# Odd mixer: a pair's two heads scored alternately from the two halves of the array's rows, values stationary and scaled probabilities moving

## The reference, cut to what matters

```python
def odd_mixer(xn, w_in, w_o, cos_f, sin_f):
    hcat = (xn @ w_in).reshape(b, s, DIL_GROUPS, 3, DIL_HEADS, HEAD_DIM)
    q = apply_rope(hcat[:, :, :, 0], cos_f, sin_f)
    k = apply_rope(hcat[:, :, :, 1], cos_f, sin_f)
    v = hcat[:, :, :, 2]
    return dilated_attention(q, k, v) @ w_o
# dilated_attention, per group: sc = q.k * HEAD_DIM**-0.5 where the key is in the
# window, e = exp(sc - m), z = sum e, o = (e / z) v, lse = m + log z;
# out = sum over the groups of softmax(lse) * o
```

## Time and profile before

| | |
|---|---|
| device time, median of 3 runs | 1459.98 us |
| profiled execution, span from the first instruction to the last | 1458.9 us; of its own time outside the span nothing is given |
| PE busy | 1340.8 us (92%), 7187 matmuls |
| PEld busy | 1102.4 us (76%) |
| DVE, ACT, POOL busy | 745.2 us (51%), 494.0 us (34%), 77.4 us (5%) |
| chain that ended last | PE 80%, DVE 11%, issue 4%, ACT 3%, DMA 2% |
| mean granted clock of PE | 0.941 of full speed |
| odd mixer's pairs with attention woven in | 975 us to 1208 us |
| attention of the last pair alone | to 1227.8 us |
| output product | 1233.4 us to 1261.1 us |

### The profile page before, as it was taken

One profiled execution on the slowest core, in us unless ns is written; L12 is line 12 of the kernel. 1 busy time (PEld: TensorE's weight loads), 2 busy tenths in 40 slices (PEclk: granted clock), 3 DMA queues, 4 the chain that ended last, 5 costly groups with the idle time before them and its releaser, 6 DMA issues.

```text
span 1458.9 us, 18192 instructions
## 1 busy us (share of the span) xinstructions
PE 1340.8 (92%) x7187; PEld 1102.4 (76%) x7187; DVE 745.2 (51%) x951; ACT 494.0 (34%) x703; POOL 77.4 (5%) x53
## 2 busy tenths in 40 slices
PE   3998997887999997989899999899999998899997
PEld 3645455554999984658489998899999997499996
DVE  4625437834555533143365546666666654365553
ACT  2152010114334332034343333454545444243331
POOL 0000045400000005000000000000000000000000
PEclk9889997769999997977999999999999997999999
DMA  9604374407565553060255563464444433445520
GB/s 330 227 0 146 108 250 156 147 3 216 175 195 172 183 162 76 0 223 8 86 203 183 172 207 102 116 163 130 124 125 124 113 116 130 173 173 177 199 86 29
DMA packets 200060, 208.17 MB, mean 143 GB/s; under 512 B 5339, under 2 KB 166502, under 8 KB 199814
## 3 DMA queue, kind: packets, MB, share of 16 engines
q1 hardware_dynamic: 196992, 201.34, 43.2%
q0 software_dynamic: 992, 3.57, 1.0%
q10 hardware_dynamic: 2022, 2.50, 0.5%
HBM read 206.35 MB, written 2.00 MB: 143 GB/s over the span
## 4 chain that ended last, share of the span: by engine, by line
PE 80%; DVE 11%; issue 4%; ACT 3%; DMA 2%; DVEq 0%; ACTq 0%; SPq 0%
PE bank L1541 16%; PE bank L1542 16%; PE bank L1543 16%; PE bank L1501 6%; PE bank L1400 6%; PE bank L1601 2%; DMA weight_pool<-in_mod_w_dram 2%; PE bank L1389 2%; PE bank L1342 2%; PE bank L1777 1%; PE bank L1660 1%; PE bank L1668 1%; DVE work L1160 1%; PE bank L1677 1%; PE bank L1592 1%
## 5 line engine op out<-in xcount | busy, mean ns | idle before, releaser
L1541 PE MATMUL bank<-hT_high,mlp_up_high 128*128 128x256 f32 x512 | 145.1, 283 | 4.8 <-DVE hT_low L854 4.8
L1543 PE MATMUL bank<-hT_high,mlp_up_low 128*128 128x256 f32 x512 | 144.9, 283 | 0.0
L1542 PE MATMUL bank<-hT_low,mlp_up_high 128*128 128x256 f32 x512 | 144.9, 283 | 0.0
L1541 PE MATMUL bank<-od_w_high,hT_high 128*128 128x384 f32 x384 | 131.8, 343 | 1.7 <-DVE hT_low L854 1.7
L1543 PE MATMUL bank<-od_w_high,hT_low 128*128 128x384 f32 x384 | 129.1, 336 | 0.0
L1542 PE MATMUL bank<-od_w_low,hT_high 128*128 128x384 f32 x384 | 129.0, 336 | 0.0
L854 DVE TENSOR_TENSOR od_w_low<-weight_pool,od_w_high 128x3072 fp32r<-128x3072 f32 x24 | 80.6, 3358 | 53.5 <-ACT od_w_high L544 53.5
L854 DVE TENSOR_TENSOR mlp_down_low<-weight_pool,mlp_down_high 128x2048 fp32r<-128x2048 f32 x32 | 73.3, 2290 | 59.1 <-ACT mlp_down_high L544 59.1
L1541 PEld LDWEIGHTS bank<-hT_high,mlp_up_high 128*128 128x128 f32 x512 | 98.1, 192 | 7.0 <-issue 3.5
L1541 PE MATMUL bank<-hT_high,ffn_up_high 128*128 128x256 f32 x352 | 99.9, 284 | 1.5 <-DVE hT_low L854 1.5
L1541 PE MATMUL bank<-mlp_down_high,hidden_high 128*128 128x512 f32 x256 | 100.3, 392 | 0.0
(11 more groups left out here) (258 smaller groups left out, 2617.8 us busy)
## 6 DMA issues: line engine op xcount, KB each, us to landing
weight_pool<-in_mlp_w_dram SPq DMA_DIRECT2D x64, 1024.0 KB, 7.5
weight_pool<-in_od_w_in_dram SPq DMA_DIRECT2D x72, 512.0 KB, 5.2
weight_pool<-in_mod_w_dram SPq DMA_DIRECT2D x12, 2048.0 KB, 8.1
weight_pool<-in_ffn_w_in_dram SPq DMA_DIRECT2D x44, 512.0 KB, 5.2
weight_pool<-in_ffn_w_out_dram SPq DMA_DIRECT2D x22, 512.0 KB, 6.0
weight_pool<-in_gla_w_in_dram SPq DMA_DIRECT2D x4, 2048.0 KB, 7.9
weight_pool<-in_gla_w_in_dram SPq DMA_DIRECT2D x4, 1024.0 KB, 11.1
weight_pool<-in_gla_w_out_dram SPq DMA_DIRECT2D x2, 2048.0 KB, 8.6
```

The source lines that it names most:

```text
L1541: mm(out_, left[0], right[0], start=start, stop=False, **flag)
L1542: mm(out_, left[0], right[1], start=False, stop=False, **flag)
L1543: return mm(out_, left[1], right[0], start=False, stop=stop, **flag)
```

## The change

- A block of scores now does both heads of one tile: for each of the three key ranges first head 0 (array rows 0 to 63, bank 3), then head 1 (rows 64 to 127, bank 4). Units are renumbered: h = j % 2, t = j // 2. Both banks must be free before a block.
- DVE scales the probabilities in place before they are turned: `od_scale`, a reciprocal of one sum and a multiplication of 128 x 512, with a semaphore `prob_scaled` for which PE's transposes wait.
- In `od_attend` the values of one head (64 columns) are stationary and the turned probabilities (128 columns) move; head 0's result goes to partitions 0 to 63 and head 1's to 64 to 127 of bank 7, so the mixer's result stands with channels on partitions. One call does both heads of a tile; it waits for both turned units. `pv_ps` counts two for a pair, where it counted four.
- `od_out` is one copy of 128 x 256 from bank 7 into `odT`, in the order of the tokens. The transposes of `om`, their copies and the waits for them go; the output product reads `odT`.

```diff
+        odT = view(work, 12800, KD, SEQ)
...
-            def turned_unit(u, j):
+            def turned_unit(u, j, free):
                 act.wait_ge(s["pT_ps"], u + 1)
-                if not isinstance(u, int) or u >= 2:
-                    act.wait_ge(s["pv_ps"], u - 1)
+                if free is not None:
+                    act.wait_ge(s["pv_ps"], free)
...
-                    turned_unit(u + 0, 0)
-                    turned_unit(u + 1, 1)
+                    turned_unit(u + 0, 0, 2 * n + U_OD)
+                    turned_unit(u + 1, 1, 2 * n + U_OD)
                     exp_unit(u + 2, 2, 1, 1.0, od_col(pn, 2))
                     exp_unit(u + 3, 3, 1, 1.0, od_col(pn, 3))
...
-                    turned_unit(u + 2, 2)
-                    turned_unit(u + 3, 3)
+                    turned_unit(u + 2, 2, 2 * n + (U_OD + 1))
+                    turned_unit(u + 3, 3, 2 * n + (U_OD + 1))
...
-            turn_evac(2, oT, dilated)
+            act.wait_ge(s["pv_ps"], U_OD + 2 * OD_PAIRS)
...
-            def od_out(n, par):
-                dve.wait_ge(s["pv_ps"], 4 * n + (U_OD + 4))
-                chain(dve.reciprocal(rinv[:, 32 + 4 * par:36 + 4 * par], rsum[:, 32 + 4 * par:36 + 4 * par]))
-                for t in range(NT):
-                    ins = dve.tensor_tensor(om5[:, t, n, :, :], bank[7][:, P * t:P * t + P].rearrange("p (h d) -> p h d", d=HD),
-                                            rinv[:, 32 + 4 * par + 2 * t:34 + 4 * par + 2 * t].unsqueeze(2).to_broadcast([P, 2, HD]),
-                                            ALU.mult)
-                ins.then_inc(s["o_out"], 1)
+            def od_scale(u, par, j):
+
+                dve.wait_ge(s["prob_ready"], u + 1)
+                col = 32 + 4 * par + j
+                chain(dve.reciprocal(rinv[:, col:col + 1], rsum[:, col:col + 1]))
+                dve.tensor_scalar(prob[:, j % 2, :], prob[:, j % 2, :], rinv[:, col:col + 1], None, ALU.mult)\
+                   .then_inc(s["prob_scaled"], 1)
+
+            def od_out(n):
+                dve.wait_ge(s["pv_ps"], 2 * n + (U_OD + 2))
+                dve.tensor_copy(dilated(odT[:, n, :]), by_sma(bank[7][:, 0:SEQ])).then_inc(s["o_out"], 1)
...
                     od_max(u + 0, 0)
                     od_max(u + 1, 1)
+                    od_scale(u + 0, pn, 0)
+                    od_scale(u + 1, pn, 1)
...
                     od_max(u + 2, 2)
                     od_max(u + 3, 3)
+                    od_scale(u + 2, pn, 2)
+                    od_scale(u + 3, pn, 3)
...
-            def od_scores(u, par, j):
-
-                pe.wait_ge(s["prob_ready"], u - 1)
-                h, t = j // 2, j % 2
-                lo = HD * h
+            def od_scores(u, par, t):
+
+                pe.wait_ge(s["prob_ready"], u)
                 for g, (at, k0, n) in enumerate([(0, 256, 256), (256, 256 + P * t, P), (384, 256 + P * t, P)]):
-                    ins = mm(bank[3 + j % 2][:, at:at + n], qkT[lo:lo + HD, par, g, P * t:P * t + P], qkT[lo:lo + HD, par, g, k0:k0 + n],
-                             start=True, stop=True)
-                ins.then_inc(s["s_ps"], 1)
-
-            def od_attend(u, par, j, n):
-                pe.wait_ge(s["pT_ready"], u + 1)
-                if j == 0:
+                    for h in range(2):
+                        lo = HD * h
+                        ins = mm(bank[3 + h][:, at:at + n], qkT[lo:lo + HD, par, g, P * t:P * t + P], qkT[lo:lo + HD, par, g, k0:k0 + n],
+                                 start=True, stop=True)
+                        if g == 2:
+                            ins.then_inc(s["s_ps"], 1)
+
+            def od_turn_probs(u, j):
+                pe.wait_ge(s["prob_scaled"], u - (U_OD - 1))
+                pe.wait_ge(s["pT_ready"], u - 1)
+                for b in range(4):
+                    ins = pe.transpose(bank[5 + j % 2][:, P * b:P * b + P], prob[:, j % 2, P * b:P * b + P], ident)
+                ins.then_inc(s["pT_ps"], 1)
+
+            def od_attend(u, par, t, n):
+                pe.wait_ge(s["pT_ready"], u + 2)
+                if t == 0:
                     pe.wait_ge(s["o_out"], n + 4)
-                h, t = j // 2, j % 2
                 for b, (g, tile) in enumerate([(0, 0), (0, 1), (1, t), (2, t)]):
-                    ins = mm(bank[7][:, P * t + HD * h:P * t + HD * h + HD], probT[:, j % 2, P * b:P * b + P],
-                             vO[:, par, g, tile, HD * h:HD * h + HD], start=(b == 0), stop=(b == 3))
+                    for h in range(2):
+                        lo = HD * h
+                        ins = mm(bank[7][lo:lo + HD, P * t:P * t + P], vO[:, par, g, tile, lo:lo + HD],
+                                 probT[:, h, P * b:P * b + P], start=(b == 0), stop=(b == 3))
                 ins.then_inc(s["pv_ps"], 1)
...
                     pe.wait_ge(s["qkT_out"], 3 * n + 3)
                     od_scores(u + 0, pn, 0)
-                    od_scores(u + 1, pn, 1)
                 if m is not None:
                     od_turn(m, pm, 0)
                     od_proj(m, pm, 2, 0)
                 if n is not None:
-                    turn_probs(u + 0, 0, u + 1)
-                    turn_probs(u + 1, 1, u + 2)
-                    od_scores(u + 2, pn, 2)
-                    od_scores(u + 3, pn, 3)
+                    od_turn_probs(u + 0, 0)
+                    od_turn_probs(u + 1, 1)
+                    od_scores(u + 2, pn, 1)
                 if m is not None:
                     od_proj(m, pm, 2, 1)
                 if n is not None:
                     od_attend(u + 0, pn, 0, n)
-                    od_attend(u + 1, pn, 1, n)
-                    turn_probs(u + 2, 2, u + 3)
-                    turn_probs(u + 3, 3, u + 4)
+                    od_turn_probs(u + 2, 2)
+                    od_turn_probs(u + 3, 3)
                 if m is not None:
                     od_turn(m, pm, 1)
                 if n is not None:
-                    od_attend(u + 2, pn, 2, n)
-                    od_attend(u + 3, pn, 3, n)
+                    od_attend(u + 2, pn, 1, n)
...
-            turn_mixed(2, om)
-            out_product(2, [("oo", 0), ("oo", 1)], oT)
+            out_product(2, [("oo", 0), ("oo", 1)], odT)
```

More of the change, by code:

```diff
@@ L246, in program @@
             mk_ps mk_out mv_ps mv_out mq_ps mq_rot mqT_ps mqT_out bias_ready
-            s_ps max_ready prob_ready pT_ps pT_ready pv_ps o_out
+            s_ps max_ready prob_ready prob_scaled pT_ps pT_ready pv_ps o_out
             od_ps od_raw od_v rot_ready qkT_ps qkT_out out_ready
@@ L692, in _ @@
                 if u >= 1:
-                    turned_unit(u - 1, u - 1)
+                    turned_unit(u - 1, u - 1, u - 2 if u >= 3 else None)
             turn_evac(1, oT, by_sma)
@@ L746, in od_values @@
                 if g == 0 and t == 0:
-                    act.wait_ge(s["pv_ps"], 4 * m + (U_OD - 4))
+                    act.wait_ge(s["pv_ps"], 2 * m + (U_OD - 2))
                 if not isinstance(m, int) or m or g:
@@ L757, in od_col @@
             def od_col(par, j):
-                return lambda h: rsum[:, 32 + 4 * par + 2 * (j % 2) + j // 2:33 + 4 * par + 2 * (j % 2) + j // 2]
+                return lambda _: rsum[:, 32 + 4 * par + j:33 + 4 * par + j]
             def od_pair(m, n, pm, pn):
@@ L1245, in od_max @@
             def od_max(u, j):
-                neg_max(u, j, None, 1, HD ** -0.5, omask[:, j % 2, :].unsqueeze(1))
-            om5 = om.rearrange("p t (n h d) -> p t n h d", h=2, d=HD)
-            def od_out(n, par):
-                dve.wait_ge(s["pv_ps"], 4 * n + (U_OD + 4))
-                chain(dve.reciprocal(rinv[:, 32 + 4 * par:36 + 4 * par], rsum[:, 32 + 4 * par:36 + 4 * par]))
-                for t in range(NT):
-                    ins = dve.tensor_tensor(om5[:, t, n, :, :], bank[7][:, P * t:P * t + P].rearrange("p (h d) -> p h d", d=HD),
-                                            rinv[:, 32 + 4 * par + 2 * t:34 + 4 * par + 2 * t].unsqueeze(2).to_broadcast([P, 2, HD]),
-                                            ALU.mult)
-                ins.then_inc(s["o_out"], 1)
+                neg_max(u, j, None, 1, HD ** -0.5, omask[:, j // 2, :].unsqueeze(1))
+            def od_scale(u, par, j):
[7 more added lines that the diff above has]
+                dve.tensor_copy(dilated(odT[:, n, :]), by_sma(bank[7][:, 0:SEQ])).then_inc(s["o_out"], 1)
             def od_pair(m, n, pm, pn):
@@ L1280, in od_pair @@
                 if n is not None:
-                    od_out(n, pn)
+                    od_out(n)
             od_pair(0, None, 0, None)
             with dve.Fori(0, OD_PAIRS // 2 - 1) as i:
-                chain.enter(i, 2 * (6 * 2 + 4 + 1))
+                chain.enter(i, 2 * (6 * 2 + 4 + 4))
                 od_pair(2 * i + 1, 2 * i, 1, 0)
@@ L1495, in out_product @@
             def out_product(n, keys, srcT):
-                pe.wait_ge(s["ogT_act"], 2 * n + 2)
-                pe.wait_ge(s["ogT_dve"], 2 * n + 2)
+                if n < 2:
```

(4 more changed lines are left out.)

## The result

In 20 runs each the changed kernel takes 1462.41 us (median), the kernel before 1458.3; the ratio is 1.0025, with a 95% interval of 1.0014 to 1.0036. Run again beside its variants it was 1463.36 against 1460.2, ratio 1.0028 (1.0012 to 1.0043). So it is slower by a quarter of a per cent, some 4 us, half of what was forecast. The profiled execution spans 1459.8 us.

What follows compares the result with a forecast made beforehand. DVE and ACT were taken to bound each pair up to `turn_probs` of unit 3, PE the rest. Terms of 0.0 plus 8 for clock falls on the profiled 1458.9 gave 1467, as median 1468.0; range 1453 to 1481.

Steps and rivals of the forecast that it cites:

- six pairs at full clock: Pairs before m = 7, clock held: scaling and attend lengthen each by 0.75 us, together +4.5 (+1.5 to +9.6).
- falls of the clock in the pairs: PE's wider wait brings the granted clock down in three to four of six pairs, 2.3 us each, +8.
- pair m = 7: This pair makes no next weights and has no such wait, so PE's saving counts: -1.4 us (-2.2 to -0.7).
- last pair alone: Attention of pair 7 alone, mostly at half clock: 18.7 us against 18.46, +0.2 (-1.5 to +2).
- turning the result: Between last attend and output product: 5.62 us of reciprocal, multiplications, transposes and copies shrink to one copy, -5.0.
- low clock in the output product: The output product now begins at half clock: 0 to 3.4 of its 27.7 us back, taken as +1.7.
- Attend, values stationary: PE's 16 attend passes with 128 columns moving and 64 loaded: 1.45 us, between bounds 0.97 and 1.94.
- Scores: A two-head block of 12 passes on PE: 1.4 us instead of 1.95, the saving worth nothing in the six pairs.
- drain at a change of tiling mode: TensorE drains when split blocks switch tiling; trace bears out 0.03 us, 0.1 a switch would add 1.4 to the sum.
- Scaling: DVE's reciprocal of 0.178 and multiplication of 0.45 us; free for units 0 and 1, 0.69 on unit 3's late chain.
- The wait: PE stands 2.7 us until the scaled unit 2, then 0.45 before unit 3 and 0.45 before attend.
- A rival's sum: Rival with no overlap in the array and clock held: attend 1.94, six pairs +1.4 each, +6.4, 1466; chance 0.10.

## Why the prediction was half right

The direction and the mechanism held: slower, PE's saving swallowed by the chain of `od_high`, `od_low` and the maxima, the scaling on that chain, the clock falling in the wider wait. The forecast of 1468 is 0.55% above the median of before that it started from, the measured loss 0.25%. What failed is the size of terms of the sum, the first of them what attend and scores cost PE. In the profiled executions:

| term | forecast, us | measured, us |
|---|---|---|
| six pairs at full clock | +4.5 | 6 x (37.50 - 37.12) = +2.3 |
| falls of the clock in the pairs | 3.5 x 2.3 = +8 | 232.4 - 222.7 less 2.3 = +7.4 |
| pair m = 7 | -1.4 | 17.44 - 19.98 = -2.5 |
| last pair alone | +0.2 | 16.9 - 18.5 = -1.6 |
| turning the result | -5.0 | 0.66 - 5.62 = -5.0 |
| low clock in the output product | +1.7 | +2.7 |
| sum | +8.0 | +3.3 |

- **Attend, values stationary** is the first mis-sized step. I bounded it by 0.97 and 1.94 and took the middle, 1.45, for no reason but that it was the middle. It took 1.03 (1209.0 to 1210.0 in the chain), at the end of full overlap: the loss of a pair with its clock held is 0.38 and not 0.75, and pair m = 7 gains 2.5. Scores, where I took 1.4 from the pace of attend's passes, took 1.08 for the same reason. That pace, 0.123 a pass, was misread besides: the transposes at 1056.61, to which I measured, had waited for an exponential that ended at 1056.56 (the line of ACT above). Where nothing is waited for, 16 of those passes take 1.73 us (1203.31 to 1205.04 in the chain of before), 0.108 each.
- **The last pair alone** is the second: I took all blocks in it at half clock, scores 2.8 and attend 2.9. They took 2.06 and 2.00. Both are at half clock, so this is the overlap again; besides, the clock was back at 1.00 from 1223.3 to 1226.8.
- **Page against row.** The Trainium skill's rule that products in different row groups run beside each other (TensorE: Matmul & The Clock Gate, "Part 3: Packing small matmuls") came out: 1.08 us is 0.55 of 1.95, and with the heads in turn most of it is lost again (1.61). The drain at a change of tiling mode that the Trainium skill names (TensorEngine Tiling (Array Packing), "Key Properties") changed no term of the sum; no run here isolates it, and the 0.1 us for a switch that I tried was assumed, not read.
- **Scaling** was right: 0.486 and 0.159 for the reciprocal, against 0.45 and 0.18. The wait was forecast at 2.7, 0.45 and 0.45, measured 3.41, 0.25 and, with the clock held, 0.25. The first is longer by the overlap once more, which brings PE there sooner.
- **The clock** was right in kind, and near in sum by luck, as two errors cancelled: six falls where I had 3.5, 1.2 us each where I had 2.3. I had taken the 6.8 us of an earlier fall for the rule; they lasted 3.4 us in four pairs, which cost 0.6 to 1.1 us each against 37.50, and 6.8 in two, which cost 1.9 and 2.0.
- **A rival's sum** was off too: without overlap a pair would have got 59.95 + 1.94 - 60.66 = 1.2 us longer, not 1.4, and the case 1465.
- Outside the odd mixer the profiled execution of after was 2.2 us shorter already at the mixer's start (919.7 against 921.9), where nothing had been changed. So its span says +0.9 and the runs +4.

## What to carry to other kernels

Before making an engine faster, follow its last small wait back: 0.66 us in six places looked like nothing and meant that every microsecond saved ahead of it would be lost, until the weights of the next pair were moved behind the maxima. Work saved ahead of such a wait was not neutral: it lengthened PE's idle stretch, and the low clock that came of it cost 1.2 us a pair in one kernel here and 3.9 in another. A few surplus passes in the stretch tell in one run how much of a loss is the clock's; the larger gain was in the order. And look at a loop's first turn apart from the others: the same move cost 4.1 us there.

## What the runs showed that I had not expected

- A wait of 1.84 us with another of 0.20, between an attend and transposes, brought the granted clock to 0.50 for 10.2 us and cost 3.9 us a pair (41.0 against 37.14), more than the wait of 3.41 us in the changed kernel (1.2 a pair, low for 3.4 to 6.8). Dense projection passes in the wait held it at 1.00 in both. The cost follows how long the clock stays low: in the one pair of that kernel with a low stretch of 3.4 us it was 1.0 us. Why it stayed low for 10.2 us in the others is not settled, and the length of the wait alone doesn't tell whether it falls: with 2.54 and 0.66 us it fell in six pairs of six, with 2.12 and 0.25 in two, with 1.84 and 0.20 behind attends of 64 columns in six.
- Column halves overlap as well as row halves: 16 passes of 128 columns on 64-column tiles take 1.09 us in turn and 1.58 us one half after the other.
